# Latent attention in a two-block fp32 network: the k and q columns in turn, half of them inside the head loop, and the rope tables made one stage earlier

## The chip, the cores and the metric

One core of one Trainium2 chip. The metric is the device time of one execution, in microseconds (us), median of the runs shown. TensorE (PE) runs matmuls and transposes; VectorE (DVE), ScalarE (ACT) and GpSimd (POOL) do the rest of the arithmetic; SyncE (SP) issues the loads of weights.

## The reference

Two transformer-like blocks on 512 tokens of width 1024, all in fp32. The first is retention with a pooling mixer and a convolutional FFN. The second has two layers: an S5 state space mixer with a SwiGLU FFN (here "the second FFN", stage f2), then latent attention with another SwiGLU FFN (stage f3). The change is in the attention and in f2. What the attention computes:

```python
def mla_shared_kv(h, w_kv_a, kv_a_norm, w_kv_b, k_nope_norm, k_rope_norm, cos, sin):
    ckv = h @ w_kv_a                                        # 512 x (256 + 32)
    c_kv = rms_norm(ckv[..., :KV_LORA_RANK], kv_a_norm)
    k_rope = apply_rope(rms_norm(ckv[..., KV_LORA_RANK:], k_rope_norm), cos, sin)
    kv = (c_kv @ w_kv_b).reshape(bsz, seq, N_HEADS, QK_NOPE_DIM + V_DIM)    # 16 heads, 64 + 64
    k_nope = rms_norm(kv[..., :QK_NOPE_DIM], k_nope_norm)
    v = kv[..., QK_NOPE_DIM:]
...
def mla_queries(h, w_q_a, q_a_norm, w_q_b, q_nope_norm, q_rope_norm, cos, sin):
    c_q = rms_norm(h @ w_q_a, q_a_norm)                     # 512 x 384
    q = (c_q @ w_q_b).reshape(bsz, seq, N_HEADS, QK_DIM)    # 16 heads, 64 + 32
    q_nope = rms_norm(q[..., :QK_NOPE_DIM], q_nope_norm)
    q_rope = apply_rope(rms_norm(q[..., QK_NOPE_DIM:], q_rope_norm), ...)
...
# causal softmax attention per head, then x = x + o @ w_o, then the SwiGLU FFN
```

The angles of the rope tables depend on the input positions, so cos and sin are made on the chip.

## The kernel before

**Split products.** Every fp32 product is made of three matmuls: each operand is split into a high part, rounded to the fp32r format, and the low rest; PE adds high x high, high x low and low x high. Weights come in chunks of up to 1024 columns per partition: SP loads a chunk into one of six slots of `w_raw` (L891 to L895), ScalarE rounds it into `w_hi` (L936, and L931 scales it by a norm's gain for kv_a and q_a), GpSimd makes `w_lo` (L865). ScalarE has no list of its own for the chunks: `ahead(count)` (L921) makes them up to four past the chunk that the next result to be read belongs to, so a chunk waits when ScalarE waits for something else. SP waits for the slot's last user, six chunks back. GpSimd takes chunks in order and has one other job in this stage, the rotation of q of groups 0 and 2 (`rope_queries`, L853), put behind a given chunk (L868).

**Order.** Each engine has its own program in order. PE's order rules: every product or transpose opens the next of eight PSUM banks in turn (`open_bank`, L311) and waits until the one that had it eight openings before was released. The engines wait for each other by semaphores alone.

**The stage around the change.** After f2 the rows are normalised and transposed (stage "mla", L1208 and L1832). Then, in PE's order (L719 to L785):

- kv_a (288 columns, four token blocks one after the other, `rows_by_tile`, four chunks of two row blocks) and q_a (384 columns, four chunks, `rows_product`). VectorE first makes the angles of the rope tables (L1833 to L1840, helpers to L1463) and ScalarE their Sin (L1210 to L1212). VectorE then copies each result into SBUF (L1842, L1851), ScalarE takes Square, sum and Sqrt of the copy (L1213 to L1228), VectorE scales it (L1845 to L1857).
- The latents are transposed (`turn_rows`, L724 and L727), multiplied by a gain, split into `a_hi` and `a_lo` (L1229, L1230; L1858, L1859). VectorE makes `q_trig` (L1861) and the shared rope part of k (L1869 to L1879).
- kv_b: four column groups of 512, one for four heads each; then q_b: four groups of 384 (L729 to L735). A group is 24 or 36 matmuls in four banks. For each group and token block (i = 0 to 31), ScalarE writes Square into one of two buffers `sq` and copies k or q out (L1258, L1260); VectorE sums the squares and, for kv, copies v (L1916 to L1923). When a group's sums are there, ScalarE takes the Sqrt (`row_deviations`, L1232) and VectorE normalises the group (`normalised(n)`, L1881); for q it waits for GpSimd's rotation or does the rotation itself (groups 1 and 3, L833). Both are called a few steps into the next group.
- The head loop (L774 to L785). Heads 0 and 1 are transposed (`head_turn`, which waits for `qk_rows`, the count of normalised groups), head 0 gets its scores. Then for each head h and token block t PE does the scores of head h + 1 and the transposes of the probabilities of head h; then `head_turn(h + 2)` and `head_out(h)`. That opens eleven banks a head. VectorE masks and takes the maximum (L1935), copies three of four transposed blocks (L1950), the k of head h + 2 (L1928), and divides the output (L1958); ScalarE takes Exp (L1274), copies the fourth block (L1290) and the q of head h + 2 (L1269).
- The output `o_n` is transposed and multiplied by `w_o`.

In f2, the gate and value columns of step f are two products of 24 matmuls; VectorE multiplies them in `swiglu` (L1816), ScalarE takes Silu (L1029).

## Time and profile before

| | us |
|---|---|
| median of 3 runs (1954.29 to 1962.46) | 1956.29 |
| the profiled execution | 1960.23 |
| its span, first to last instruction | 1958.4 |
| PE busy | 1821.8 (93%) |
| DVE busy | 814.4 (42%) |
| ACT busy | 651.4 (33%) |
| POOL busy | 679.7 (35%) |

The mean granted clock of TensorE is 0.96 of full speed. The profile names engines by the short names in brackets above; PEld is PE's weight load. A row of a timeline has the start, the duration, the engine, the line, the operation with output <- input and shape, how many were merged (x4), and in brackets the idle time of that engine before it with what ended it. A matmul's duration includes its way through the array; the next one starts before it is over, so the distance between two starts is what it costs. Row durations of DVE, ACT and POOL overlap by some 0.1 us as well.

### The profile page before, as it was taken

To read this page: it belongs to the slowest core of one execution; us is meant where nothing else is said; L and a number is where in the kernel's file an instruction comes from. 1 tells how busy PE (TensorE), PEld (TensorE's weight loads), DVE (VectorE), ACT (ScalarE), POOL (GpSimd) and SP (SyncE) were. 2 spreads that over 40 slices of the span, in tenths; PEclk is the share of its full clock that TensorE was granted. 3 is DMA by queue.
4 is the path that set the end of the run, shared out by engine and by line. 5 is a ranking of instruction groups with operands and counts; after the bars stand their busy time and mean duration, and the time that the engine had idled before them with its cause. 6 is when DMAs were issued, how large, how long until landed. Compare 5 with 4: busy or idle time off the path is not lost.

```text
span 1958.4 us, 22658 instructions
## 1 busy us (share of the span) xinstructions
PE 1821.8 (93%) x9038; PEld 1522.5 (78%) x9038; DVE 814.4 (42%) x1445; ACT 651.4 (33%) x1102; POOL 679.7 (35%) x300
## 2 busy tenths in 40 slices
PE   6789999999999589999999999998879999999999
PEld 5677787788787468878988888877858898888887
DVE  1587579769755524522311110125676331111111
ACT  1223135335253232232422222236555343223121
POOL 1432234434343330024344344423510134534442
PEclk8899999999999788999999999998989999999999
DMA  9221234454545344622333323212300133333322
GB/s 214 60 76 55 86 90 152 125 164 134 166 121 167 115 151 153 238 89 86 98 97 97 97 86 108 92 57 80 93 1 1 44 87 97 96 97 92 102 91 81
DMA packets 234215, 202.71 MB, mean 104 GB/s; under 512 B 38912, under 2 KB 194688, under 8 KB 232064
## 3 DMA queue, kind: packets, MB, share of 16 engines
q1 hardware_dynamic: 198272, 170.29, 28.5%
q10 hardware_dynamic: 35840, 30.98, 5.2%
q8 instruction: 73, 1.20, 0.3%
q14 instruction: 30, 0.25, 0.0%
HBM read 175.55 MB, written 25.69 MB: 103 GB/s over the span
## 4 chain that ended last, share of the span: by engine, by line
PE 75%; DVE 14%; DMA 3%; ACT 3%; ACTq 2%; issue 2%; POOL 1%; SPq 1%; DVEq 0%; POOLq 0%
PE ps L347 11%; PE ps L349 11%; PE ps L348 11%; PE ps L371 9%; PE ps L373 9%; PE ps L372 9%; DMA rec<-s_records 2%; PE ps L750 2%; PE ps L769 2%; PE ps L402 1%; PE ps L404 1%; PE ps L403 1%; PE ps L666 1%; DVE x_rows L1437 1%; PE ps L760 1%
## 5 line engine op out<-in xcount | busy, mean ns | idle before, releaser
L865 POOL TENSOR_TENSOR w_lo<-w_raw,w_hi 128x1024 fp32r<-128x1024 f32 (+4 forms) x284 | 668.7, 2365 | 1238.6 <-ACT w_hi L936 1238.3
L347 PE MATMUL ps<-a_hi,w_hi 128*128 128x512 f32 (+1 forms) x1184 | 443.7, 375 | 10.5 <-DVE q_t L1585 6.1
L348 PE MATMUL ps<-a_lo,w_hi 128*128 128x512 f32 (+1 forms) x1184 | 441.8, 373 | 0.0
L349 PE MATMUL ps<-a_hi,w_lo 128*128 128x512 f32 (+1 forms) x1184 | 441.7, 373 | 0.0
L936 ACT ACTIVATE w_hi<-w_raw 128x1024 fp32r<-128x1024 f32 (+4 forms) x284 | 283.8, 1016 | 320.2 <-DMA w_raw<-in_ffn_w_gate_up_dram 72.8
L347 PEld LDWEIGHTS ps<-a_hi,w_hi 128*128 128x128 f32 x1184 | 224.0, 189 | 51.8 <-issue 6.8
L349 PEld LDWEIGHTS ps<-a_hi,w_lo 128*128 128x128 f32 x1184 | 223.9, 189 | 39.0
L348 PEld LDWEIGHTS ps<-a_lo,w_hi 128*128 128x128 f32 x1184 | 223.9, 189 | 38.7
L371 PE MATMUL ps<-w_hi,a_hi 128*128 128x512 f32 (+1 forms) x432 | 172.1, 398 | 39.3 <-POOL w_lo L865 18.8
L1821 DVE TENSOR_TENSOR ev<-ps,xh 128x512 f32<-128x512 f32 x44 | 30.4, 692 | 417.4 <-PE ps L349 407.4
L371 PE MATMUL ps<-w_hi,h_hi 128*128 128x512 f32 x476 | 190.4, 400 | 9.0 <-DVE x_rows L1410 4.9
L373 PE MATMUL ps<-w_hi,h_lo 128*128 128x512 f32 x476 | 189.2, 397 | 0.0
L372 PE MATMUL ps<-w_lo,h_hi 128*128 128x512 f32 x476 | 189.2, 397 | 0.0
L372 PE MATMUL ps<-w_lo,a_hi 128*128 128x512 f32 (+1 forms) x432 | 170.4, 394 | 0.0
L373 PE MATMUL ps<-w_hi,a_lo 128*128 128x512 f32 (+1 forms) x432 | 170.2, 394 | 0.0
L1410 DVE TENSOR_TENSOR x_rows<-ps,x_rows 128x512 f32<-128x512 f32 x72 | 49.2, 691 | 233.4 <-PE ps L373 193.3
L371 PEld LDWEIGHTS ps<-w_hi,a_hi 128*128 128x128 f32 x432 | 86.0, 199 | 56.2 <-issue 24.7
L371 PEld LDWEIGHTS ps<-w_hi,h_hi 128*128 128x128 f32 x476 | 90.1, 189 | 33.0 <-issue 8.1
L952 ACT ACTIVATE h_hi<-ev 128x512 fp32r<-128x512 f32 x66 | 41.5, 629 | 209.7 <-DVE ev L1821 195.5
L373 PEld LDWEIGHTS ps<-w_hi,h_lo 128*128 128x128 f32 x476 | 90.1, 189 | 21.8
L372 PEld LDWEIGHTS ps<-w_lo,h_hi 128*128 128x128 f32 x476 | 90.2, 190 | 21.3
L373 PEld LDWEIGHTS ps<-w_hi,a_lo 128*128 128x128 f32 x432 | 85.4, 198 | 15.1
(334 smaller groups left out, 2241.9 us busy)
## 6 DMA issues: line engine op xcount, KB each, us to landing
w_raw<-in_ffn_w_gate_up_dram SPq DMA_DIRECT2D x88, 512.0 KB, 3.8
rec<-s_records ACTq DMA_DIRECT2D x16, 1440.0 KB, 6.3
w_raw<-in_w_up_dram SPq DMA_DIRECT2D x44, 512.0 KB, 4.0
w_raw<-in_ffn_w_down_dram SPq DMA_DIRECT2D x40, 512.0 KB, 3.6
s_records<-stage SPq DMA_DIRECT2D x16, 928.0 KB, 6.2
w_raw<-in_w_in_dram SPq DMA_DIRECT2D x20, 512.0 KB, 4.1
w_raw<-in_w_down_dram SPq DMA_DIRECT2D x20, 512.0 KB, 4.2
w_raw<-in_ssm_w_glu_dram SPq DMA_DIRECT2D x16, 512.0 KB, 3.6
```

Source lines behind the costliest of these rows:

```text
L347: pe.matmul(bank, wh, xh_, start=first, stop=False)
L348: pe.matmul(bank, wh, xl_, start=False, stop=False)
L349: return pe.matmul(bank, wl, xh_, start=False, stop=last)
L371: pe.matmul(o, ah[:, k + kk, s], wh[:, kk, :], start=(n == 0 and kk == 0), stop=False)
L372: pe.matmul(o, ah[:, k + kk, s], wl[:, kk, :], start=False, stop=False)
L373: m = pe.matmul(o, al[:, k + kk, s], wh[:, kk, :], start=False, stop=end)
L750: m = pe.matmul(b[:, 0:(t + 1) * P], qk_t[:, h % 2, 0, t * P:t * P + P], qk_t[:, h % 2, 1, 0:(t + 1) * P], start=True, stop=True)
L769: m = pe.matmul(b[:, t * VD:t * VD + VD], p_t[:, o:o + P], v_n[:, j, h, :], start=(j == 0), stop=(j == t))
L865: pool.tensor_tensor(w_lo[:, n % RING, 0:w], w_raw[:, n % RING, 0:w], w_hi[:, n % RING, 0:w].bitcast(F), ALU.subtract).then_inc(lo_made, 1)
L936: act.activation(w_hi[:, n % RING, 0:w], w_raw[:, n % RING, 0:w], ACT.Copy).then_inc(hi_made, 1)
L952: act.activation(hi, view(ev[:, i % 2, :]), ACT.Copy).then_inc(hi_ready, 1)
L1410: ins = v.tensor_tensor(o, b, o, ALU.add)
```

## The change

- kv_a is taken in chunks of three row blocks. Its and q_a's results are read from PSUM by ScalarE and VectorE, without the copies in between.
- The angles are made by VectorE in f2 before step 4, Sin by ScalarE before step 6, and `q_trig` by VectorE before step 10. The shared rope part of k is made after the sums of kv_b's group 0.
- kv_b and q_b are taken in turn, group by group; groups 0 and 1 before the heads. Groups 2 and 3 are cut into 16 pieces of one token block (`column_piece`), in the order kv 2, q 2, kv 3, q 3; two of them in each of heads 0 to 7, the first after the second score block, the second before `head_out`. A head with pieces opens thirteen banks. ScalarE's evictions and VectorE's sums follow suit; the Sqrt of a late group comes in heads 2, 4, 6 and 8 ahead of the first piece's eviction, its normalisation at the end of the same head.
- `head_turn(h)` waits for the two normalised groups of its own four heads and those before.
- GpSimd rotates q of group 0 behind the third chunk after q_b 0, and q of group 2 behind the next one.
- The latents lie in blocks 0 to 4 of `a_hi` and 3 to 7 of `a_lo`, and `o_n` is laid out by pairs of heads over the other blocks.

```diff
+EARLY = 2
+PIECES = 2
...
-            rows_by_tile(("kv_a",), mla_w_kv_a_2, a_hi, a_lo, KT, 0, KVR + ROPE, 2, gain=0, wait_t=mla[1],
+            rows_by_tile(("kv_a",), mla_w_kv_a_2, a_hi, a_lo, KT, 0, KVR + ROPE, 3, gain=0, wait_t=mla[1],
...
+            for c in range(EARLY):
+                columns(0, c)
+                columns(1, c)
...
+            def column_piece(i):
+                n, t = divmod(i, TT)
+                if n >= 2 * HC:
+                    return
+                c, q = divmod(n, 2)
+                nk, cn, at_k = (QR // P, HN * QK, 2) if q else (KVR // P, HALF, 0)
+                w = mla_w_q_b_2[0] if q else mla_w_kv_b_2
+                b = open_bank(((("kv_b", "q_b")[q]), c, t))
+                if t == 0:
+                    piece_parts[:] = [take_chunk(rows_of(w, k, min(2, nk - k), c * cn, cn), min(2, nk - k), cn)
+                                      for k in range(0, nk, 2)]
...
             def head_turn(h):
-                pe.wait_ge(qk_rows, HC + h // HN + 1)
+                pe.wait_ge(qk_rows, 2 * (h // HN + 1))
...
                     head_probs(h, t)
+                    if t == 1:
+                        column_piece(2 * EARLY * TT + PIECES * h)
                 if h + 2 < NH:
                     head_turn(h + 2)
+                column_piece(2 * EARLY * TT + PIECES * h + 1)
                 head_out(h)
...
-                    if n == chunks_at[("q_b", c, 0)] + 2:
+                    if n == chunks_at[("q_b", c, 0)] + (3 if c < EARLY else 1):
                         rope_queries(c)
...
+                        if (stage, f) == ("f2", 6):
+                            rope_trig()
...
+            for i in range(2 * EARLY * TT):
+                evict_piece(i)
+                if i % TT == 1 and i > TT:
+                    row_deviations(i // TT - 1)
...
                     if h + 1 < NH:
                         exponentials(h + 1, t)
+                n, t = divmod(2 * EARLY * TT + PIECES * h, TT)
+                if t == 0 and 2 * EARLY < n <= 2 * HC:
+                    row_deviations(n - 1)
+                evict_piece(2 * EARLY * TT + PIECES * h)
                 if h:
                     act.wait_ge(*closed(("o", h - 1)))
                 b = full(act, ("pt", h, TT - 1))
                 release(("pt", h, TT - 1), act.activation(p_t[:, tri(TT - 1)], b, ACT.Copy))
                 if h + 2 < NH:
                     q_turned(h + 2)
+                evict_piece(2 * EARLY * TT + PIECES * h + 1)
...
+                        if (stage, f) == ("f2", 4):
+                            rope_angles()
+                        if (stage, f) == ("f2", 10):
+                            rope_factors()
...
             for t in range(TT):
-                w = release(("q_a", t), v.tensor_copy(cq[:, t, :], full(v, ("q_a", t))[:, 0:QR]))
-                v.wait_ge(*w)
-                v.memset(st[:, 190:191], 0.0).then_inc(lat_in, 1)
-            for t in range(TT):
-                v.wait_ge(lat_dev, TT + t + 1)
+                b = full(v, ("q_a", t))
+                v.wait_ge(lat_dev, 2 * TT + t + 1)
                 step(v.reciprocal(st[:, 48 + t:49 + t], st[:, 40 + t:41 + t]))
-                v.tensor_scalar(cq[:, t, :], cq[:, t, :], st[:, 48 + t:49 + t], None, ALU.mult).then_inc(cq_ready, 1)
+                release(("q_a", t), v.tensor_scalar(cq[:, t, :], b[:, 0:QR], st[:, 48 + t:49 + t], None, ALU.mult))
...
+            for i in range(2 * EARLY * TT):
+                piece_sums(i)
+                if i % TT == 2 and i > TT:
+                    normalised(i // TT - 1)
+                if i == TT - 1:
+                    k_rope()
...
-            normalised(2 * HC - 1)
+            normalised(2 * EARLY - 1)
...
+                piece_sums(2 * EARLY * TT + PIECES * h)
                 if h + 2 < NH:
                     k_turned(h + 2)
...
                 v.wait_ge(*w)
+                piece_sums(2 * EARLY * TT + PIECES * h + 1)
+                n, t = divmod(2 * EARLY * TT + PIECES * h, TT)
+                if t == 0 and 2 * EARLY < n <= 2 * HC:
+                    normalised(n - 1)
```

## Rows read from the trace of the kernel before

**Rows 1.** Busy time in stretches: engines (instructions), then granted clock, DMA share, GB/s.

```profile
1310.53:1445.42 134.89, 104.10 (x539) 93.83 (x538) 83.80 (x209) 75.74 (x186) 54.20 (x34) 0.86 0.23 70
1445.42:1531.60 86.18, 86.18 (x619) 72.88 (x618) 57.69 (x193) 47.52 (x136) 0.00 (x0) 1.00 0.01 2
```

**Rows 2.** Timeline of DVE, second FFN: start, duration, work, [idle before <- releaser].

```profile
1022.58 0.69 DVE L1821 TENSOR_TENSOR ev<-ps,xh 128x512 f32<-128x512 f32 x1 [9.59 <-PE ps L349]
```

**Rows 3.** Timeline of PE, 1310 to 1445 us, where it had been idle.

```profile
1316.13 0.37 PE L402 MATMUL ps<-w_hi,a_hi 128*128 128x288 f32 x1 [2.78 <-ACT w_hi L936]
...
1334.16 0.66 PE L371 MATMUL ps<-w_hi,a_hi 128*128 128x384 f32 x1 [3.80 <-POOL w_lo L865]
...
1359.58 0.77 PE L371 MATMUL ps<-w_hi,a_hi 128*128 128x512 f32 x1 [3.63 <-DVE ev L1356]
...
1399.68 0.66 PE L371 MATMUL ps<-w_hi,a_hi 128*128 128x384 f32 x1 [3.20 <-POOL w_lo L865]
...
1430.10 5.03 PE L750 MATMUL ps<-qk_t 96*128 96x128 f32 x10 [13.21 <-issue]
...
1441.34 0.61 PE L742 MATMUL ps<-ident,q_n 128*96 128x128 f32 x4 [2.52 <-ACT prob L1274]
```

**Rows 4.** Busy time and granted clock (1.00 is full) right after two restarts.

```profile
1316.74:1320.01 3.27, 2.86 (x13) 2.53 (x12) 1.20 (x2) 0.30 (x1) 0.83 (x1) 0.52 0.02 5
1400.14:1405.58 5.44, 5.44 (x19) 5.44 (x19) 2.40 (x4) 0.00 (x0) 4.53 (x3) 0.50 0.04 12
```

**Rows 5.** Timelines of POOL, PE and ACT: prices of one instruction.

```profile
1314.58 1.41 POOL L865 TENSOR_TENSOR w_lo<-w_raw,w_hi 128x576 fp32r<-128x576 f32 x1 [12.16 <-ACT w_hi L936]
...
1387.13 0.33 PE L372 MATMUL ps<-w_lo,a_hi 128*128 128x384 f32 x1
1387.30 0.33 PE L373 MATMUL ps<-w_hi,a_lo 128*128 128x384 f32 x1
...
1374.49 0.38 ACT L1258 ACTIVATE xh<-ps 128x256 f32<-128x256 f32 x1 [0.29 <-PE ps L373]
1374.77 0.38 ACT L1260 ACTIVATE k_n<-ps 128x256 f32<-128x256 f32 x1
1375.85 0.38 ACT L1258 ACTIVATE xh<-ps 128x256 f32<-128x256 f32 x1 [0.70 <-PE ps L373]
...
1354.12 1.04 ACT L936 ACTIVATE w_hi<-w_raw 128x1024 fp32r<-128x1024 f32 x1
...
1392.23 1.48 POOL L837 TENSOR_TENSOR q_rot<-q_n,q_trig 128x256 f32<-128x256 f32 x1 [6.06 <-ACT q_n L1260]
```

**Rows 6.** Timeline of ACT: a table load and the Sqrt behind it.

```profile
1328.32 1.28 ACT L1219 ACT_TABLE_LOAD   x1
1329.62 0.30 ACT L1219 ACTIVATE st<-st,eps_c 128x1 f32<-128x1 f32 x1
```

**Rows 7.** Timeline of DVE: the last normalisation of a q group.

```profile
1435.86 1.23 DVE L1896 TENSOR_TENSOR q_n<-q_n,xh 128x1024 f32<-128x1024 f32 x1
1437.00 0.42 DVE L837 TENSOR_TENSOR q_rot<-q_n,q_trig 128x256 f32<-128x256 f32 x1
...
1439.75 0.69 DVE L1903 TENSOR_TENSOR q_n<-q_n,xh 128x512 f32<-128x512 f32 x1
```

**Rows 8.** Timelines of PE and ACT in a settled head.

```profile
1464.55 0.44 PE L750 MATMUL ps<-qk_t 96*128 96x128 f32 x2
...
1466.57 1.02 PE L750 MATMUL ps<-qk_t 96*128 96x512 f32 x2
...
1468.74 2.34 PE L769 MATMUL ps<-v_n,p_t 128*128 128x64 f32 x20
1470.92 0.44 PE L750 MATMUL ps<-qk_t 96*128 96x128 f32 x2
...
1468.42 0.69 ACT L1274 ACTIVATE prob<-ps,st 128x512 f32<-128x512 f32 x1 [0.65 <-DVE st L1935]
...
1469.10 0.59 ACT L1290 ACTIVATE p_t<-ps 128x512 f32<-128x512 f32 x1
```

More of the change, by code:

```diff
@@ L193, in program @@
         rot = scratch("rot", [P, 2, NH, ROPE // 2], F, 81)
-        o_n = nc.alloc_sbuf_tensor_at("o_n", [P, TT, NH * VD], F, offset=base + 32 * KB)
+        o_n = nc.alloc_sbuf_tensor_at("o_n", [P, NH // 2, TT, 2 * VD], F, offset=base + 26 * KB)
+        c_hi, c_lo = a_hi[:, 0:5, :], a_lo[:, 3:8, :]
         qk_t = scratch("qk_t", [QK, 2, 2, SEQ], F, 64)
@@ L725, in _ @@
                       ready=lambda t: pe.wait_ge(ckv_ready, t + 1), through_ev=True)
-            kv_split = n_split[0] - TT
+            cq_split = n_split[0]
             turn_rows("cq_t", lambda t, k: cq[:, t, k * P:k * P + P], QR // P,
-                      ready=lambda t: pe.wait_ge(cq_ready, t + 1), through_ev=True)
-            for c in range(HC):
-                rows_product(("kv_b", c), mla_w_kv_b_2, a_hi, a_lo, KVR // P, c * HALF, HALF, 2,
-                             wait_t=(lambda t, k: kv_split + t + 1) if c == 0 else None)
@@ L732, in _, with columns @@
-            pe.wait_ge(lo_ready, n_split[0])
-            for c in range(HC):
-                rows_product(("q_b", c), mla_w_q_b_2[0], a_hi[:, 2:5, :], a_lo[:, 2:5, :], QR // P,
-                             c * HN * QK, HN * QK, 2)
+                      ready=lambda t: pe.wait_ge(*freed[bank_no[("q_a", t)]]), through_ev=True)
+            def columns(q, c):
+                if q:
+                    rows_product(("q_b", c), mla_w_q_b_2[0], c_hi[:, 2:5, :], c_lo[:, 2:5, :], QR // P,
+                                 c * HN * QK, HN * QK, 2, wait_t=(lambda t, k: cq_split + t + 1) if c == 0 else None)
+                else:
+                    rows_product(("kv_b", c), mla_w_kv_b_2, c_hi, c_lo, KVR // P, c * HALF, HALF, 2,
+                                 wait_t=(lambda t, k: kv_split + t + 1) if c == 0 else None)
@@ new lines, in _ @@
+            for c in range(EARLY):
+                columns(0, c)
+                columns(1, c)
+            piece_parts = []
+            def column_piece(i):
[9 more added lines that the diff above has]
+                                      for k in range(0, nk, 2)]
+                for k, (wh, wl) in zip(range(0, nk, 2), piece_parts):
+                    kn = min(2, nk - k)
+                    for kk in range(kn):
+                        s = slice(t * P, t * P + P)
+                        end = k + kk == nk - 1
+                        ah, al = c_hi[:, at_k + k + kk, s], c_lo[:, at_k + k + kk, s]
+                        pe.matmul(b[:, 0:cn], ah, wh[:, kk, :], start=(k + kk == 0), stop=False)
+                        pe.matmul(b[:, 0:cn], ah, wl[:, kk, :], start=False, stop=False)
+                        m = pe.matmul(b[:, 0:cn], al, wh[:, kk, :], start=False, stop=end)
+                    if t == TT - 1 and not end:
+                        chunk_over(m)
+                over = close_bank(((("kv_b", "q_b")[q]), c, t), m)
+                if t == TT - 1:
+                    chunk_done.append(over)
```

136 lines of the change are left out of this document (66 added, 70 removed).

## The prediction

> **What bounds the kernel now.** I read the busy time of the engines in stretches first. Between 1310.53 us, where the transposes of the third token block for the attention part begin, and 1445.42 us, where the loop over heads has settled, PE is busy for 104.10 of 134.89 us, so 30.8 us are idle; from there to 1531.60 us it has no idle time at all, at a granted clock of 1.00 [rows 1]. Elsewhere the change touches only the second FFN, where VectorE idles 9.59 us in each column step [rows 2]. So the question is how much of the 30.8 us goes and what the settled loop gives back.
>
> The timeline of PE shows where it is idle [rows 3]: 2.78 us before the third chunk of kv_a, 3.80 before q_a, 3.63 before kv_b, 3.20 inside q_b behind GpSimd's w_lo, 13.21 before the first scores, then 2.52; the small rest is 1.7. After each of the first five PE runs at the lower of its two clock levels. 3.27 us at a granted 0.52 after the first lose 3.27 x 0.48 = 1.6 us, 5.44 us at 0.50 after the fourth lose 2.7 [rows 4]; I take 1.6 each for the second and third too, and half of the 5.03 us of ten scores after the fifth [rows 3], 2.5. Together 10.0 us. Idle and slow time come to 40.8 us: **kv_a** 3.2 + 1.6 = 4.8, **q_a** 3.8 + 1.6 = 5.4, **kv_b** 4.1 + 1.6 = 5.7, **q_b** 3.2 + 2.7 = 5.9, **start of the heads** 16.5 + 2.5 = 19.0. PE's work itself is the same in both kernels: the same products and transposes, in another order. So the sum is 40.8 less what idle and slow time remain.
>
> **The change part by part.**
> *kv_a in chunks of three.* ScalarE makes two chunks before the norm of this stage, now six of eight row blocks. PE lasts 2.4 us on them (18 matmuls of 288 columns, estimated at 0.13 us from the 0.17 of 384 [rows 5]). The last chunk is made where the third was: its w_lo ends with the row at 1314.58 and its 1.41 us [rows 5], at 1316.0. PE waits 2.1 us instead of 3.2, under the 2.52 us that cost no clock [rows 3]. Remains 2.1.
>
> *Rope tables into the second FFN, kv_a and q_a read from PSUM.* In the old place VectorE made the angles before it copied kv_a, and ScalarE waited behind it with the weight chunks of q_a queued: that is the 3.80 us. Now the q_a chunks are split while kv_a runs, and nothing remains. In the FFN, some 3 us of small VectorE work fall into the 9.59 us [rows 2]; on ScalarE two table loads of 1.28 us [rows 6] and two Sin; PE is five banks and four weight chunks ahead there, so I cost it at nothing. Without that cover it would be 3 to 6 us. SP and GpSimd are moved past nothing here.
>
> *The latents.* The copies of q_a out of PSUM go, but Square, Sqrt, scaling, gain and split still follow q_a's last matmul in series, and kv_b's four banks need four gain steps. The wait shrinks by 0.4 us. Remains 3.7 + 1.6 = 5.3.
>
> *k and q of a group in turn.* The 3.20 us were GpSimd's rotation queued ahead of the weight split for q_b. It now comes after the split of the second group's last chunk and starts when q_b of group 0 is evicted; PE has 11.6 us of kv_b and q_b of group 1 to run by then (24 matmuls of 1.36/6 = 0.227, 36 of 0.173 [rows 5]). Remains nothing. The rotation itself takes 5.6 us, six steps of which the first is the row at 1392.23 [rows 5].
>
> *Start of the heads.* PE does groups 0 and 1 in 2 x (5.4 + 6.2) = 23.2 us, 25.2 with the slow start. Counting VectorE from kv_b's start: latents split 5.1; sums and v of kv_b to 7.9; the shared rope key (3.3) when the last tile is in, to 12.1; q_b 0 and the first normalisation to 17.1; kv_b 1, then q of group 0, which waits for GpSimd until 20.9, to 23; q_b 1, k of group 1 and two k_turned to 29.4. PE is ready for scores at 27.0: wait 1.7. Then q of group 1 is normalised on VectorE: 1.2 + 6 x 0.44 + 0.7 and reciprocals = 5.0 us [rows 7], with masks of head 1 behind it. With the extra piece in the bank order, the last transpose of head 0 needs a bank that head 1's first exp frees: PE waits 2.7 us at 34.7, and before the output of head 0 another 1.9 for head 1's last exp, the split of a weight chunk (1.04 us [rows 5]) and the piece's eviction. Remains 6.3 instead of 19.0.
>
> *Pieces in heads 0 to 7.* PE has 16 pieces more there (1.36 us for kv, 36/4 x 0.173 = 1.55 for q), moved, not added. A settled head takes 6.37 us of PE, and its tightest chain is scores from 1466.57, mask, exp at 1468.42, copy of p_t 1469.10 to about 1469.6, against the last part of the output at 1469.8 [rows 8]: 0.3 us to spare. A piece adds 1.4 us of cover, but the output's bank is the one of the head's first piece, so it waits for that eviction: exp, Square, Copy (0.28 us apart [rows 5]), on kv also VectorE's sum and copy. That is 2.7 us after the last scores against 2.67 of PE work: no wait in a plain head. In heads 2, 4, 6 and 8 ScalarE first takes the Sqrt of the row sums. That needs another table. The load takes 1.28 us and Sqrt follows 0.02 us later [rows 6]; with the Sqrt itself 1.6 us for k, 1.95 for q. It stands before the eviction, and in heads 2, 4 and 6 a weight split of 0.95 (1.04 less the overlap with its neighbour), or 0.75 for a smaller chunk, stands there too. Waits: head 2 1.9, head 4 (kv, through VectorE) 2.9, head 6 2.0, head 8 1.7. VectorE's normalisations add after head 4 (2.1 us) 1.2, and after head 8 (5.0, with its own rotation [rows 7], no piece to cover) 4.0. Sum **13.7**. The load back to the Exp table falls beside the output product and I cost it at nothing; uncovered it would be 1.3 in each of four heads. Three waits of 2.7 and more may cost clock, as 2.78 did [rows 3, 4]: some 1.0 each, **3.0**. This case's trace never shows Sqrt between Exps, nor eviction between heads. Bounds: all of it hidden, 0, as the settled loop's idle time is [rows 1]; double the waits, 33.4. I take 16.7, as it is counted from rows near by.
>
> A page of the Trainium skill speaks against the change: ScalarE: Activation LUTs, section What ACT_TABLE_LOAD costs, has a drain of about 1.38 us beside each load, 2.66 us for a switch. By that the four switches in the heads would cost 5.5 us more, and the time would be 1951.4. The 0.02 us from load to Sqrt [rows 6] speak for the load alone.
>
> *The o_n layout and the use of other blocks of a_hi and a_lo* change addresses only; same sizes, same counts: nothing. SP's queue has the chunks of kv_b and q_b in another order and one chunk fewer; each is asked for six chunks ahead.
>
> **Sum.** Remaining: 2.1 + 0 + 5.3 + 0 + 6.3 + 16.7 = 30.4; gain 40.8 - 30.4 = 10.4 us. The profiled execution took 1960.23 us, 1.8 more than its span and 3.9 above the median of 1956.29. It would take 1949.8; against the median, 1945.9.
>
> **The rivals.**
> A, *the heads hide it all*: PE has 2.9 us more per head and the other engines run ahead. For: no idle time from 1445.42 to 1531.60 [rows 1]; against: 0.3 us to spare [rows 8]. Gain 27.1, time 1929.2. Chance 0.22.
> B, *given back*: waits in the heads twice as long (ordinary heads wait 0.5 to 1 us for the bank too, the load back to Exp isn't hidden). 1945.9 + 16.7 = 1962.6. Chance 0.15.
> C, *slower*: the output of each of the eight piece heads waits for the whole serial chain of mask, exp, eviction, sum and copy, 3.3 us, plus a weight split of 1, with nothing beside it. 8 x 4.3 = 34.4, less the 8.0 that I count in heads 2, 4, 5 and 6: 1945.9 + 26.4 = 1972.3. It decides from 3.5 us a head on: 8 x 3.5 - 8.0 = 20.0, which is what lies between the forecast and 0.5% above the median, 1966.1. For: the tight chain; against: evictions are pipelined 0.28 us apart [rows 5]. Chance 0.06.
> D, *a table switch costs more than its load*: if ScalarE stood idle around a switch once more for as long as the load takes, 1.28 us [rows 6], that would come four times on the chain of the heads, 5.1 us, 1951.0. For: the row is a switch after a Square, not after an Exp; against: it shows a gap of 0.02. Chance 0.04. The page on the activation tables, named above, makes that wait 1.38.
> That the change doesn't do what it says is excluded by its loops: all eight pieces of each late group are issued in heads 0 to 7.
>
> **How the numbers follow.** The forecast has 0.53, between 1938 and 1956 by its unknown terms. To leave out no more than 2 in 10, the range goes to A below, a little past its middle, and to half of B above: 1928 to 1961. A change under 0.5% (9.8 us) can't be told from none here; the bound is 1946.5, and the forecast lies on it. Faster: 0.22 of A and 0.31 of the forecast, 0.53. Same: 0.22 of the forecast, B and D, 0.41. Slower: 0.06.
>
> **What would show it.** PE idle before q_a and inside q_b gone, at most 2.2 us in kv_a, some 3.6 still before kv_b; the wait before the first scores 1 to 3 us instead of 13.21; heads 1, 3 and 7 about 9.2 us apart without idle time; table loads in heads 2, 4, 6 and 8, with PE idle 1.7 to 3 us before the output product; a wait of some 3 us in head 9. No new wait in the second FFN. The forecast is wrong if the settled heads with pieces show idle time everywhere, or the Sqrt heads none.

## The result, and the profile after

The kernel with the change takes **1967.37 us** (median of 13 runs, 1962.25 to 1974.71), the kernel before 1956.29 (13 runs, 1950.51 to 1962.46): a ratio of 1.0059 with a 95% interval of 1.0043 to 1.0075. It is slower by about 11 us. I had forecast 1945.9 and a range of 1928 to 1961.

The profiled execution took 1962.25 us. The page of the kernel after, its span, busy times and two of the lines in 40 slices:

```profile
span 1960.4 us, 22648 instructions
...
PE 1825.8 (93%) x9038; PEld 1522.4 (78%) x9038; DVE 809.0 (41%) x1433; ACT 657.6 (34%) x1107; POOL 676.9 (35%) x299
...
PE   6789989999998599999999999999888999999999
...
PEclk8899999999999788999999999999889999999999
```

The page says little: 93% busy, as before, and three slices at 8 where the heads are. And the whole time is a poor measure here, because the part of the program ahead of the attention varies by itself: kv_a's first matmul starts at 1311.52 us in the profile of before, at 1303.42 in that of after, and between 1300.34 and 1311.27 in the profiles of the experiments, of which only one touches that part (rope tables back). So I measure **the stage**: from kv_a's first matmul to the first matmul of w_o. Busy time in that stretch, before and then after with its parts (columns as in [rows 1]):

```profile
1311.52:1542.87 231.35, 199.04 (x1229) 175.04 (x1229) 146.17 (x414) 128.59 (x334) 54.20 (x34) 0.92 0.14 43
```

```profile
1303.42:1544.83 241.41, 210.33 (x1229) 181.31 (x1229) 136.54 (x383) 132.91 (x335) 49.51 (x33) 0.91 0.13 40
1303.42:1376.74 73.32, 62.20 (x357) 58.31 (x357) 42.49 (x96) 45.19 (x116) 30.70 (x20) 0.95 0.28 78
1376.74:1393.88 17.14, 15.13 (x67) 11.00 (x67) 11.56 (x34) 8.42 (x24) 0.00 (x0) 0.80 0.00 1
1393.88:1451.93 58.05, 47.40 (x246) 39.92 (x246) 23.61 (x74) 26.17 (x65) 11.77 (x10) 0.82 0.09 28
1451.93:1508.00 56.07, 50.28 (x297) 41.17 (x298) 36.60 (x111) 33.62 (x79) 7.04 (x3) 0.91 0.09 29
1508.00:1544.83 36.83, 35.31 (x269) 30.91 (x267) 22.29 (x70) 19.51 (x52) 0.00 (x0) 1.00 0.04 15
```

The same 1229 matmul rows, 241.41 us against 231.35: the stage is 10.1 us longer, which is the result. Idle time fell a little (32.3 to 31.1 us), but the matmuls themselves take 11.3 us more, at a granted clock of 0.82 and 0.91 in the two stretches that hold turns 1 to 9 of the head loop. Before, the heads ran at 1.00.

The timeline of PE where it had been idle, kernel after: first the part ahead of the heads, then the heads.

```profile
1308.03 0.37 PE L403 MATMUL ps<-w_hi,a_hi 128*128 128x288 f32 x1 [1.99 <-POOL w_lo L905]
...
1321.94 0.41 PE L372 MATMUL ps<-w_hi,a_hi 128*128 128x384 f32 x1 [0.95 <-DVE ckv L1917]
...
1371.31 0.64 PE L779 MATMUL ps<-ident,q_n 128*96 128x128 f32 x4 [0.78 <-DVE q_n L1963]
1376.74 4.93 PE L787 MATMUL ps<-qk_t 96*128 96x128 f32 x10 [3.48 <-ACT qk_t L1317]
1387.88 0.63 PE L797 MATMUL ps<-ident,prob 128*128 128x128 f32 x4 [1.19 <-ACT prob L1322]
1391.60 2.44 PE L806 MATMUL ps<-v_n,p_t 128*128 128x64 f32 x20 [0.81 <-DVE v_n L1984]
...
1414.32 4.47 PE L806 MATMUL ps<-v_n,p_t 128*128 128x64 f32 x20 [1.88 <-ACT q_n L1304]
...
1436.46 0.77 PE L765 MATMUL ps<-w_hi,a_hi 128*128 128x512 f32 x1 [5.83 <-POOL w_lo L905]
...
1448.04 4.11 PE L806 MATMUL ps<-v_n,p_t 128*128 128x64 f32 x20 [2.92 <-DVE v_n L1984]
...
1472.73 2.44 PE L806 MATMUL ps<-v_n,p_t 128*128 128x64 f32 x20 [2.10 <-ACT q_n L1304]
...
1492.02 1.18 PE L806 MATMUL ps<-v_n,p_t 128*128 128x64 f32 x8 [1.83 <-ACT p_t L1342]
```

Beside these stand the wait before kv_b (3.78 us) and three under 0.9 in head 9. Of the waits of [rows 3], the 3.80 before q_a shrank to 0.95, the 3.20 inside q_b is gone, the 13.21 before the first scores is 3.48. In heads 2, 4, 6 and 8 PE waits 1.88, 2.92, 2.10 and 1.83 us before the output product, where I had counted 1.9, 2.9, 2.0 and 1.7. And there is one that I had not: **5.83 us in head 4, behind GpSimd's w_lo**. The timeline of POOL just before it:

```profile
1429.24 0.73 POOL L877 TENSOR_TENSOR q_rot<-q_n,q_trig 128x256 f32<-128x256 f32 x1 [55.36 <-ACT q_n L1304]
...
1433.29 0.73 POOL L882 TENSOR_TENSOR q_n<-q_n,q_rot 128x256 f32<-128x256 f32 x1
1433.97 5.08 POOL L905 TENSOR_TENSOR w_lo<-w_raw,w_hi 128x1024 fp32r<-128x1024 f32 x3
```

GpSimd stood idle for 55.36 us, rotated q of group 2 once ScalarE had evicted its last piece, and only then split the weights of kv_b group 3, for which PE was waiting. `rope_queries(2)` stands behind chunk `chunks_at[("q_b", 2, 0)] + 1`, and that is the last chunk of q_b 2 itself, ahead of kv_b 3's. PE couldn't go on to the scores of head 5, so VectorE and ScalarE waited too (the row at 1441.33 below, 9.04 us). The timeline of ScalarE, around the Sqrt of head 2 and behind that stall:

```profile
1411.17 1.28 ACT L1282 ACT_TABLE_LOAD   x1
1412.47 0.31 ACT L1282 ACTIVATE xh<-xh,eps_c 128x16 f32<-128x16 f32 x1
1412.68 0.83 ACT L976 ACTIVATE w_hi<-w_raw 128x768 fp32r<-128x768 f32 x1
1413.41 0.47 ACT L1302 ACTIVATE xh<-ps 128x384 f32<-128x384 f32 x1
1413.78 0.48 ACT L1304 ACTIVATE q_n<-ps 128x384 f32<-128x384 f32 x1
...
1419.40 1.28 ACT L1322 ACT_TABLE_LOAD   x1 [3.33 <-PE ps L787]
...
1441.33 0.58 ACT L1322 ACTIVATE prob<-ps,st 128x384 f32<-128x384 f32 x1 [9.04 <-DVE st L2002]
```

The order is the one that I had written down: load, Sqrt, weight split, Square, Copy, which frees the bank. The gap from load to Sqrt is 0.02 us again, and the load back to the Exp table falls beside the first scores, before the mask that the Exp needs.

### The profile page after: what moved, and what is told of

It is laid out like the page before. It is cut to its first block, busy times and chain, and to the rows that moved or that the text cites. A ratio compares the mean times of both kernels' runs of the same rounds, so it can differ in the third digit from the quotient of the medians.

```text
span 1960.4 us, 22648 instructions
## 1 busy us (share of the span) xinstructions
PE 1825.8 (93%) x9038; PEld 1522.4 (78%) x9038; DVE 809.0 (41%) x1433; ACT 657.6 (34%) x1107; POOL 676.9 (35%) x299
## 4 chain that ended last, share of the span: by engine, by line
PE 76%; DVE 12%; ACT 4%; DMA 3%; issue 2%; ACTq 2%; POOL 1%; SPq 1%; DVEq 0%; POOLq 0%
PE ps L348 12%; PE ps L349 12%; PE ps L350 12%; PE ps L372 8%; PE ps L373 8%; PE ps L374 8%; DMA rec<-s_records 2%; PE ps L806 2%; PE ps L787 2%; PE ps L403 1%; PE ps L405 1%; PE ps L404 1%; PE ps L667 1%; DVE x_rows L1490 1%; ACT w_hi L976 1%
## 5 line engine op out<-in xcount | busy, mean ns | idle before, releaser
L348 PE MATMUL ps<-a_hi,w_hi 128*128 128x512 f32 (+1 forms) x1184 | 443.9, 375 | 10.9 <-DVE q_t L1638 6.6
L372 PE MATMUL ps<-w_hi,a_hi 128*128 128x512 f32 (+1 forms) x392 | 155.0, 395 | 34.3 <-DVE a_lo L1399 12.9
L373 PE MATMUL ps<-w_lo,a_hi 128*128 128x512 f32 (+1 forms) x392 | 154.1, 393 | 0.0
L374 PE MATMUL ps<-w_hi,a_lo 128*128 128x512 f32 (+1 forms) x392 | 153.8, 392 | 0.0
L372 PEld LDWEIGHTS ps<-w_hi,a_hi 128*128 128x128 f32 x392 | 76.4, 195 | 50.3 <-issue 18.9
L374 PEld LDWEIGHTS ps<-w_hi,a_lo 128*128 128x128 f32 x392 | 76.4, 195 | 14.2
```

What stands on the lines that cost most here:

```text
L348: pe.matmul(bank, wh, xh_, start=first, stop=False)
L372: pe.matmul(o, ah[:, k + kk, s], wh[:, kk, :], start=(n == 0 and kk == 0), stop=False)
L373: pe.matmul(o, ah[:, k + kk, s], wl[:, kk, :], start=False, stop=False)
L374: m = pe.matmul(o, al[:, k + kk, s], wh[:, kk, :], start=False, stop=end)
```

## The experiments

Each median is of 6 or 12 runs (13 for the first two rows), in three groups with the kernel before beside them (medians of before 1955.57, 1956.42 and 1956.18 us); the ratio is to that of the group. "Stage" is the stretch defined above, "front" the part of it up to the first scores, and "turns" the part from the start of turn 1 of the head loop to w_o; a turn of the loop is called a head. The front shifts by 1.5 us from one profile to the next with nothing changed in it (q_a starts 17.0 or 18.5 us after kv_a; the early ones are marked *). What shifts is the clock: behind the first wait in kv_a, 1.99 us in both, PE ran at a granted 0.82 in the kernel after and at 1.00 in the next run:

```profile
1303.42:1312.80 9.38, 7.39 (x43) 7.19 (x43) 2.21 (x4) 5.75 (x11) 3.24 (x2) 0.82 0.31 87
1300.34:1308.22 7.88, 5.89 (x44) 5.68 (x44) 2.21 (x4) 5.76 (x11) 3.25 (x2) 1.00 0.33 103
```

The turns are free of this shift but not of others like it, as head 1 shows below, so a difference of one profile is good to 2 or 3 us at best. The stage is that of one profiled execution each: the median is the firmer number, and the difference of two medians can be 7 us away from that of the stages.

| kernel | median us | ratio (95% interval) | front | turns | stage | clock in stage |
|---|---|---|---|---|---|---|
| before | 1956.29 |  | 118.58 | 97.45 | 231.35 | 0.92 |
| after | 1967.37 | 1.0059 [1.0043, 1.0075] | 73.32 | 150.95 | 241.41 | 0.91 |
| rotation behind kv 3 | 1957.06 | 1.0012 [0.9994, 1.0031] | 71.80 * | 140.92 | 229.95 | 0.93 |
| Sqrt last | 1947.55 | 0.9965 [0.9947, 0.9983] | 73.31 | 137.06 | 227.50 | 0.93 |
| no table load in heads | 1944.90 | 0.9942 [0.9923, 0.9961] | 73.30 | 133.62 | 224.17 | 0.95 |
| all groups early | 1938.86 | 0.9904 [0.9881, 0.9927] | 101.95 | 99.03 | 217.11 | 0.94 |
| three groups early | 1947.03 | 0.9951 [0.9933, 0.9969] | 87.00 * | 121.39 | 223.06 | 0.93 |
| rope tables back | 1948.62 | 0.9958 [0.9941, 0.9975] | 109.55 | 97.43 | 222.91 | 0.95 |
| kv then q | 1946.43 | 0.9948 [0.9927, 0.9968] | 105.55 | 100.51 | 222.26 | 0.93 |
| late normalisation | 1937.79 | 0.9903 [0.9879, 0.9926] | 100.12 | 103.68 | 212.83 | 0.97 |
| pieces mended | 1947.20 | 0.9950 [0.9929, 0.9970] | 73.32 | 132.13 | 220.17 | 0.95 |
| late, and all rotations on GpSimd | 1932.55 | 0.9876 [0.9849, 0.9903] | 95.19 * | 102.01 | 206.23 | 0.99 |

**Rotation behind kv 3.** The changed kernel, with GpSimd's rotation of group 2 one chunk later:

```diff
-                    if n == chunks_at[("q_b", c, 0)] + (3 if c < EARLY else 1):
+                    if n == chunks_at[("q_b", c, 0)] + (3 if c < EARLY else 2):
```

> Edit: GpSimd rotates q of group 2 behind the weight split of kv_b's group 3 instead of ahead of it; nothing else. Measure: the time, and the stage from the first matmul of kv_a to the first of w_o, which took 231.4 us before and 241.4 with the change. Theory Q (queue order): in head 4 PE waited 5.83 us for that split behind the rotation, then ran at the low clock, and head 4 took 22.5 us against 9.1 of work; with the order mended that wait goes, head 4 takes 12 to 15 us, the stage 231 to 234, the time 1956 to 1960, ratio to before 1.000 to 1.002. Theory T (table loads and evictions bound the heads, the rotation's wait only came first): another wait takes its place in head 4, the stage stays over 238 and the time over 1963.

The stage fell from 241.41 to 229.95 us (231 to 234 expected). The 5.83 us wait is gone; heads 1 to 5, which took 11.1 13.6 10.8 **22.5** 11.2, became 9.4 12.4 12.1 **14.1** 11.2. Head 4 loses 8.4 us: the wait and 2.6 us of slow clock. The turns lose 10.0 (150.95 to 140.92), but the other 1.6 lies in heads 1 to 3, and heads 1 and 2 the edit doesn't reach. Head 1, the same instructions without a wait, in the kernel after and in this run:

```profile
1393.88:1404.93 11.05, 11.03 (x60) 8.87 (x60) 5.62 (x18) 4.62 (x14) 0.00 (x0) 0.85 0.11 25
1389.37:1398.81 9.44, 9.43 (x61) 7.61 (x60) 5.54 (x18) 4.62 (x14) 0.00 (x0) 1.00 0.10 27
```

The medians agree with the larger figure, 1967.37 to 1957.06 us. So a position in a queue that is wrong by one chunk is what makes the change a loss; with it mended the change is worth nothing either way, within the interval.

**Sqrt last.** On top of that, the Sqrt of a late group goes behind both evictions of its head, so that it stands ahead of nothing that PE waits for; the normalisation follows one head later.

```diff
-                n, t = divmod(2 * EARLY * TT + PIECES * h, TT)
-                if t == 0 and 2 * EARLY < n <= 2 * HC:
-                    row_deviations(n - 1)
...
                 evict_piece(2 * EARLY * TT + PIECES * h + 1)
+                n, t = divmod(2 * EARLY * TT + PIECES * h, TT)
+                if t == 0 and 2 * EARLY < n <= 2 * HC:
+                    row_deviations(n - 1)
```

> Edit: as e1, and in heads 2, 4, 6, 8 ScalarE takes the Sqrt of the row sums after both evictions and the copies of the head, VectorE normalises the group one head later. The same instructions, the two table loads included, but not ahead of the eviction that frees the output's bank. Theory T1 (the load costs by its place on the chain): the waits of 1.9, 2.9, 2.1 and 1.8 us before the output products go, and the slow clock behind the first two; 6 to 14 us less than e1, stage 219 to 227, ratio 0.994 to 0.997. Theory T2 (ScalarE is simply too full in these heads, wherever the loads stand): they come back as a wait for the first Exp of the next head, and the gain over e1 is under 3 us.

The median is 9.5 us lower and its ratio 0.9965, as theory T1 has it; the turns of the profile are only 3.9 us shorter and the stage 2.4. The split by heads explains the difference. Heads 2 to 8 take 10.5 us less and now run at full clock; heads 9 to 11 take 6.6 more (30.6 against 24.0), where a wait of 3.23 us in head 10 stands behind the last normalisation, which comes one head later and holds VectorE ahead of the masks. Heads 2 to 8 with the rotation behind kv 3, then in this run, then in the next one without table loads:

```profile
1398.81:1478.98 80.17, 71.12 (x420) 61.22 (x419) 42.20 (x132) 48.70 (x113) 14.77 (x12) 0.91 0.11 37
1404.31:1473.98 69.67, 64.61 (x420) 54.78 (x420) 42.82 (x133) 46.51 (x111) 15.60 (x12) 1.00 0.13 43
1401.03:1470.44 69.41, 64.41 (x421) 54.77 (x420) 42.30 (x133) 39.28 (x106) 14.79 (x12) 1.00 0.13 43
```

The waits before the output product fell, from 1.89 to 0.25 us in head 2, from 2.92 to 1.71 in head 4, from 2.08 to 1.29 in head 6 and from 1.83 to 0.81 in head 8. ScalarE at the end of head 2:

```profile
1413.85 1.28 ACT L1282 ACT_TABLE_LOAD   x1
1415.14 0.31 ACT L1282 ACTIVATE xh<-xh,eps_c 128x16 f32<-128x16 f32 x1
1415.47 1.28 ACT L1322 ACT_TABLE_LOAD   x1
1416.77 0.37 ACT L1322 ACTIVATE prob<-ps,st 128x128 f32<-128x128 f32 x1
```

Both loads now stand in front of the next head's Exp, which follows without idle time on ScalarE. PE waits for nothing in head 3 all the same (9.5 us), so theory T2 is not borne out.

**No table load in the heads.** Rotation behind kv 3, and Identity in place of Sqrt for the late groups, so the kernel leaves out the root in the norms of heads 8 to 15.

```diff
+                fn = ACT.Sqrt if n < 2 * EARLY else ACT.Identity
```

> Edit: as e1, but the Sqrt of the late groups (heads 2, 4, 6, 8) is left out: Identity with the same scale and bias in its place, which needs no table load, so the row norms of heads 8 to 15 are not the reference's. The waits fall to the Sqrt's own 0.3 us. Theory T: at least as fast as e2 if place is all; if e3 is faster than e2 by over 3 us, the loads cost something wherever they stand; if e3 gains under 3 us on e1, the loads never mattered and the low clock has another cause. I expect e3 6 to 15 us under e1, within 3 us of e2.

The turns take 7.3 us less than with the rotation mended (133.62 against 140.92), 1.8 for each of four switches. That is a net: heads 2 to 8 take 10.8 us less, and heads 9 to 11 give 3.5 back, in and behind a wait of 3.61 us in head 9, where VectorE normalises q of the last group ahead of the masks. In heads 2 to 8 leaving the loads out gives no more than moving them (69.41 against 69.67 us). So what costs there is their place ahead of the eviction, not the loads by themselves; by the medians the two kernels are 2.7 us apart, within the 3 that I expected. With the switches gone about half of what the pieces cost in the stage (next run) is still there.

**All groups early.** The changed kernel with `EARLY = 4`: no pieces, everything else of the change stays.

```diff
-EARLY = 2
+EARLY = 4
```

> Edit: the change with all four groups before the heads (EARLY = 4), so no pieces and no Sqrt in the head loop; k and q in turn, rope tables in the second FFN and PSUM reads stay. This is the front part of the change alone. My sum gave the front 2.7 + 5.4 + 0.4 + 5.9 us and a shorter start of the heads. Theory F (the front part gains, the pieces lose it): the stage takes 211 to 222 us and the ratio is 0.990 to 0.995. Theory G (the front saves nothing, since VectorE is behind and takes it back at the start of the heads): stage 228 or more, ratio over 0.998, with a wait of over 10 us before the first scores.

The stage is 217.11 us, 14.2 less than before, and the time 1938.86, 17 us less. This separates the change into a front that wins 14.2 us and pieces that cost 12.8 us (229.95 - 217.11) even with the queue mended, 14.3 with the shift of the front taken out, and 18.2 by the medians (1957.06 and 1938.86). Head 1 takes 8.0 us and all later ones 6.4.

**Three groups early.** `EARLY = 3`, pieces in heads 0 to 3 alone, Sqrt in heads 2 and 4.

> Three of the four column groups ahead of the heads, only the fourth as pieces, in heads 0 to 3; the rotation of group 2 then also stands behind the next group's weight splits. From the first kv_a matmul to the first one of w_o the kernel with two early groups and the order mended needs 229.95 us, the one with all four early 217.11. Theory (each piece and each Sqrt among Exps has its price): about half of the 12.8 us between them, 222 to 225 us, and 1945 to 1948 us in all; no head longer than 12.5 us behind head 1. Rival 1 (the price lies in the start, where the other engines lag and pieces come on top): 226 or more, 1949 or more. Rival 2 (what costs is that many heads in a row stay irregular and PE's clock low): under 220, under 1943.

The stage is 223.06 us (224.6 without the shift of the front), the time 1947.03: half the pieces cost half, 7.5 of 14.3 us, or 8.2 of 18.2 by the medians. The price goes with the number of pieces and switches, as the first theory says; its "no head longer than 12.5" failed, head 2 takes 13.9, after a wait of 2.09 us at a low clock.

**Rope tables back.** All groups early, with `rope_angles`, `rope_trig` and `rope_factors` called where the kernel before does that work.

```diff
-                        if (stage, f) == ("f2", 4):
-                            rope_angles()
-                        if (stage, f) == ("f2", 10):
-                            rope_factors()
...
             rms_and_split("mla", 2 * TT, to_a, add_last("f2"))
+            rope_angles()
```

> All four groups early, and the rope tables put back to where the kernel before has them: VectorE makes the angles ahead of its kv_a work, ScalarE its two Sin behind the split of the third stage, the factors behind the split of the latents. Theory (my step: the wait before q_a, 3.80 us and its low clock 1.6, comes from these tables): the wait before q_a goes from 0.97 back to about 4 us, the stretch from kv_a to w_o from 217.1 to 221 to 223 us, in all 1942.5 to 1945. Rival (it came from the copies of kv_a out of PSUM and the changed chunks, not from the tables): under 219 us, within 1.5 us of 1938.9.

The stage grows by 5.8 us, and PE's wait before q_a from 0.97 to 6.84:

```profile
1326.25 0.66 PE L372 MATMUL ps<-w_hi,a_hi 128*128 128x384 f32 x1 [6.84 <-DVE ckv L1913]
```

I had the term at 5.4 (3.8 and 1.6 of clock). The near agreement with 5.8 is in part luck. Up to kv_b's first matmul this run is 7.8 us later, 5.9 by the wait and 1.9 by the clock behind it; 2.0 in sum come back further on, by the clock: behind a wait of 2.43 us before a kv_b group it stays at 1.00, where all groups early had 0.76 behind 2.44, and head 1 runs at full clock, where it had 0.80. The median is 9.8 us above that of all groups early, 1948.62 against the 1942.5 to 1945 expected. Why the wait is longer than the 3.80 of [rows 3] I didn't test; the row names VectorE's scaling of kv_a, which now reads PSUM and frees the bank.

**kv then q.** All groups early, all of kv_b ahead of all of q_b.

```diff
-            for c in range(EARLY):
-                columns(0, c)
-                columns(1, c)
+            for q in range(2):
+                for c in range(EARLY):
+                    columns(q, c)
```

> All four groups early, but all four of kv_b first and then all four of q_b, as in the kernel before; GpSimd's rotation stays behind the weight splits of the next q group. This takes back the order alone. Theory (the order of k and q in turn gives VectorE and GpSimd time for q while PE runs kv_b): VectorE waits for the rotations with no kv_b between, and scores start 3 to 8 us later than the 101.95 us after kv_a's first matmul, the stretch to w_o is 220 to 226 us, in all 1942 to 1948. Rival 1 (the order does nothing; what the kernel before lost was GpSimd's queue and the latents): scores at 100 to 103, 215 to 219 us, 1937 to 1941. Rival 2 (the order is the whole gain): scores at 112 or later, 227 or more, 1949 or more.

The stage is 5.2 us longer, the median 7.6. The two waits before kv_b groups (1.75 and 2.44) vanish, but the one before the scores is 13.46, as large as in [rows 3]:

```profile
1412.80 1.62 PE L787 MATMUL ps<-qk_t 96*128 96x128 f32 x4 [13.46 <-issue]
```

```profile
1395.63 0.97 DVE L877 TENSOR_TENSOR q_rot<-q_n,q_trig 128x256 f32<-128x256 f32 x1
...
1401.01 2.71 DVE L1963 TENSOR_TENSOR q_n<-q_n,xh 128x512 f32<-128x512 f32 x1
...
1411.96 1.40 DVE L1995 TENSOR_SCALAR qk_t<-ps,gcol 96x512 f32<-96x512 f32 x2
```

VectorE has the sums and normalisations of three q groups in a row and is 12 us behind PE when it comes to the k of head 0. With the order alone taken back, the 13.21 us return: it is k and q in turn that makes that wait small, for 4.2 us of waits further ahead.

**Late normalisation.** All groups early; the last three of the eight normalisations go behind the outputs of heads 1, 3 and 5, and GpSimd rotates group 3 too.

```diff
-                if i % TT == 2 and i > TT:
+                if i % TT == 2 and TT < i < 6 * TT:
                     normalised(i // TT - 1)
...
-                n, t = divmod(2 * EARLY * TT + PIECES * h, TT)
-                if t == 0 and 2 * EARLY < n <= 2 * HC:
-                    normalised(n - 1)
+                if h in (1, 3, 5):
+                    normalised(5 + h // 2)
```

> All four groups early; the normalisation of the last three of the eight row sets (q of group 2, k and q of group 3) is taken out of the start and put behind the outputs of heads 1, 3 and 5 on VectorE, and GpSimd rotates group 3 too. Theory (VectorE is what PE waits for from kv_b to the first scores: 1.75, 2.44 and 3.38 us): scores start 5 to 8 us earlier than 101.95, three heads get some 1 to 2 us longer, and the stretch to w_o is 210 to 214 us, 1932 to 1936 us in all. Rival (the masks of the heads behind a normalisation come late and PE waits as long there as before, at a low clock): 216 to 220 us, 1938 to 1942.

The stage is 212.83 us, 4.3 less. The median, 1937.79, lies between the two forecasts and only 1.1 below that of all groups early, so it doesn't confirm the gain. The scores start only 1.8 us earlier, not 5 to 8: the waits of 1.73 and 2.45 us before kv_b groups are still there, since they come from earlier normalisations. The gain is the first head, 16.1 to 9.0 us, where q of the last group had stood ahead of the masks of head 1. Heads 2, 3, 4 and 6 get 0.9 to 1.9 longer.

**Pieces mended.** Sqrt last, and q of group 1 normalised behind the output of head 0, with all four rotations on GpSimd.

```diff
-                for c in range(0, HC, 2):
-                    if n == chunks_at[("q_b", c, 0)] + (3 if c < EARLY else 2):
+                for c in range(HC):
+                    if n == chunks_at[("q_b", c, 0)] + (3, 3, 2, 1)[c]:
...
-            normalised(2 * EARLY - 1)
...
+                if h == 0:
+                    normalised(2 * EARLY - 1)
```

> Pieces of groups 2 and 3 in heads 0 to 7 as in the changed kernel, with three things mended: the rotation of group 2 behind the next group's weight split, Sqrt behind both evictions (that much is the run with Sqrt last, 227.50 us from kv_a to w_o, first head 17.1 us), and now q of group 1 normalised behind the output of head 0 instead of ahead of it, with all rotations on GpSimd. Theory (the 17.1 us of the first head, against 9.3 of PE work in it, come from VectorE's normalisation of q of group 1 ahead of the masks of head 1): first head 9.5 to 12 us, two or three later ones a little longer, 219 to 223 us, 1940 to 1944 us in all; still above the 217.11 of all groups early. Rival 1 (the first head waits for ScalarE's exps, pieces and weight splits, whatever VectorE does): first head 15 us or more, 226 or more. Rival 2 (with the stalls gone the pieces hide the waits that all groups early has, and win): under 217.

The stage is 220.17 us, as expected, but the first head takes 14.7 (17.1 before the edit), near the first rival's 15. It is not that rival's wait: PE is busy for 14.70 of the 14.72 us, at a granted clock of 0.78. The time, 1947.20, is above the expected 1940 to 1944 and equal to the 1947.55 of Sqrt last, so the medians don't confirm the gain of the stage. The best form of the pieces that I tried stays behind all groups early, by 3 us of the stage and 8 of the medians; against the next run, which has the same mends and no pieces, it is 14 and 15.

**Late, and all rotations on GpSimd.** Late normalisation, and GpSimd also rotates group 1.

```diff
-                for c in (0, 2, 3):
+                for c in range(HC):
...
-                    if c == 1:
-                        go(rope_chunk(v, c, q_rot[:, 1, :, :, :, :], step))
-                    else:
-                        v.wait_ge(q_roped, (1, 0, 2, 3)[c])
+                    v.wait_ge(q_roped, c + 1)
```

> All four groups early with the late normalisation (212.83 us from kv_a to w_o, scores at 100.12), and GpSimd rotates group 1 as well, which VectorE did itself. Theory (VectorE is what PE waits for between kv_b and the scores: 1.73, 2.45 and 1.62 us): the 2.45 us before the last kv_b group shrinks to under 1, 210 to 212 us, 1935 to 1938 in all. Rival (GpSimd's rotation slows VectorE beside it and holds up the weight splits, so that the wait only changes its releaser): 212.5 to 216.

The 2.45 us wait is down to 0.55, the scores start 4.9 us earlier (1.5 of that is the shift of the front), one more head is at 6.4. Better than expected, and **the fastest kernel of the study: 1932.55 us, 0.9876 of the kernel before**, with PE at a granted clock of 0.99 in the whole stage:

```profile
1308.89:1515.12 206.23, 190.11 (x1229) 167.36 (x1229) 133.76 (x371) 122.64 (x327) 61.24 (x45) 0.99 0.15 46
```

## Why the prediction was wrong

I had the stage 10.4 us shorter; it is 10.1 longer, 20.5 us between. The runs and the trace split that:

| where | predicted | measured | miss |
|---|---|---|---|
| front, to the first scores | 69.5 | 73.32 | 3.9 |
| first head | 17.0 | 17.14 | 0.1 |
| heads after it, beyond the moved products: GpSimd's queue, in head 4 | 0 | 8.4 | 8.4 |
| the same: all else | 16.7 | 24.7 | 8.0 |

(Front: 118.58 less 23.2 for the groups moved and less the 25.9 gained by my terms up to there. First head: 15.3 before, less its 5.8 idle and slow, plus the 4.6 of waits that I counted and 2.9 for two pieces at the mean price of both sorts. Heads after it: the turns took 97.45 before; 14 pieces take 20.4 more; after has 150.95 and so 33.1 extra; head 4 gives back 8.4 with the queue mended, and the turns in all 10.0, to 140.92, so 23.1 extra there.)

**The step that failed: "Remains nothing" for GpSimd's rotation.** I checked that the rotation of group 0 now stands behind the second group's weights and let that stand for both. For group 2 the code says `+ 1` where group 0 has `+ 3`. I described that position and didn't cost it. One question would have found it: for a step that is moved, what is behind it on its queue, and who waits for that? Behind it were kv_b 3's weights, due in the same head. The price could be had: 5.6 us for the six rotation steps, as I counted them for group 0, and a w_lo of 1.41 or more [rows 5] behind the eviction, 7 to 8 us less the little that PE has left to do. The wait was 5.83 us, and head 4 took 8.4 more with it than without.

**The clock in the heads was mis-sized.** My waits were right one by one: 8.73 us measured in heads 2, 4, 6 and 8 against 8.5. For the clock behind them I had 3.0 us in all. By the stretches above the heads lose 58.05 x 0.18 + 56.07 x 0.09 = 15.5 us to it, and in the run with the queue mended the 23.1 are some 10.7 of idle time, 10.9 of slow clock and 1.5 that the pieces themselves take beyond my price (head 1 of that run, at full clock and without a wait, has 9.44 - 6.37 = 3.07 us for two kv pieces, where I had 2.7). I took 2.52 us as harmless from [rows 3]; here two waits of 1.88 and 2.92 us were each followed by an output product at half clock. In sum idle time in the heads cost about twice its length. With the Sqrt moved behind the evictions the clock came back too: heads 2 to 8 ran at 1.00 with 5 us of waits left in them.

**The front** missed 3.9: 1.8 more before the first scores, 0.95 before q_a where I had nothing, 0.78 before the transposes, and 1.5 of slow clock behind the wait in kv_a, for which I had none. These come to 5.0; smaller errors the other way make up the difference. One row that lies on that path is VectorE's scaling of the rotated q, which takes four times as long as in [rows 7] when it starts beside GpSimd's weight split (below).

**What was right.** The tables: 5.4 predicted, 5.8 measured by putting them back. The agreement is in part luck, as said there. The FFN takes them without a wait: from 900 to 1100 us PE is busy for 199.27 us in both kernels, while VectorE has 5.9 us more to do, where I had 3. The waits in kv_a (1.99 against 2.1) and before kv_b (3.78 against 3.7) stand.

**What was right by luck.** The first head, 17.14 against 17.0: PE waits for 2.0 us in it and not for 4.6, and the rest is a granted clock of 0.80, for which I had nothing. The waits after heads 4 and 8 were too high, 5.2 against 1.9.

**The rivals.** A (all hidden) is excluded: every Sqrt head waits. B's number for the heads, 33.4, is what the heads lost, 33.1, but not by its mechanism: no ordinary head waits, and the load back to Exp is hidden; it is one queue and the clock. C, the slower one, is as near in time (1972.3 against B's 1962.6), and its mechanism didn't happen: head 7 with its two pieces takes 9.5 us, no more than its products, and heads 1, 3 and 5 show no wait before their output product. A slower result had its place in the code, and I looked for it in the serial chain only. D: no second idle time around a load, 0.02 us in every one. The Trainium skill, ScalarE: Activation LUTs, section What ACT_TABLE_LOAD costs, has about 1.38 us of drain with each; these rows don't show it. Where ScalarE has work on both sides of a load, the gap is 0.02 us before it and 0.02 or less behind it, also between the Sqrt and the load back (rows of Sqrt last). The run without loads gives 1.8 us for a switch, but that is the net named above and no price of the load.

**The better plan for the change.** Its front is worth 14.2 us of the stage: 5.8 by the tables, 5.2 by the order of k and q. The other 3.2 (chunks of three, no copies, the queue of GpSimd) are a remainder that I didn't test; by the medians, 9.8 and 7.6 of some 17, nothing is left for it. Moving products into the heads costs 12.8 to 14.3 by the stage and 18 by the medians, and a good part of it, 7.1 by the stage and 6.0 by the medians, without any table switch: the heads as they were left PE no idle time [rows 1], so work put there adds its own time, and each wait that it brings comes on top. What the pieces were to hide, VectorE's lag at the start, is cheaper to remove by delaying VectorE's normalisations, which need no PE.

## What to carry to other kernels

When work is spread into a loop, list for every engine the queue position of each thing that moves with it, for each group and not just for the first: a helper's side job one slot too early stalls the product behind it for the whole chain. Put work into a loop only where its bound engine idles; one that is busy without a gap gains nothing and pays for each new wait, here about twice, as the clock was low behind several of them. And before moving the bound engine's work, try moving the work of the engine that it waits for.

## What the runs showed of the hardware

**Short waits and TensorE's clock.** Granted clock of five stretches of the kernel after: the output products of heads 2 and 3 (0.51 behind a wait of 1.88 us, then 1.00), the piece behind the 5.83 us, and the output products of heads 4 (2.92 us before it) and 6 (2.10 before it):

```profile
1414.32:1418.60 4.28, 4.28 (x21) 4.28 (x21) 1.07 (x3) 1.75 (x4) 0.00 (x0) 0.51 0.00 0
1427.74:1429.41 1.67, 1.67 (x17) 1.67 (x17) 0.25 (x2) 1.34 (x4) 0.17 (x1) 1.00 0.67 153
1436.46:1440.43 3.97, 3.97 (x9) 2.68 (x9) 0.00 (x0) 0.00 (x0) 2.59 (x2) 0.50 0.02 4
1448.04:1451.93 3.89, 3.89 (x20) 3.89 (x21) 0.68 (x2) 1.03 (x3) 1.32 (x1) 0.56 0.00 0
1472.73:1475.17 2.44, 2.44 (x21) 2.44 (x22) 1.07 (x3) 1.75 (x4) 1.61 (x1) 1.00 0.00 0
```

0.51 is the lower of the two levels (1.2 GHz), 1.00 the upper (2.4 GHz). The same product behind nearly the same wait, 1.88 and 2.10 us, ran once at either. Stronger still are the pairs of the section on the experiments: kv_a behind the same wait of 1.98 to 2.00 us ran at 0.82 in eight of the eleven profiles from the kernel after on, and at 1.00 in three; and head 1 had 0.85 and 1.00 with no wait in it. So the length of the wait alone doesn't decide, and a wait of this size has to be priced at both ends, its length and about twice that. I made no run that isolates what decides.

**VectorE beside GpSimd.** The scaling of the rotated q, with 512 columns from two inputs in SBUF, takes 0.69 us alone and 2.87 when it starts beside GpSimd's weight split. Kernel after, VectorE and then GpSimd:

```profile
1368.38 2.87 DVE L1963 TENSOR_TENSOR q_n<-q_n,xh 128x512 f32<-128x512 f32 x1 [0.63 <-POOL q_n L882]
...
1386.29 0.69 DVE L1963 TENSOR_TENSOR q_n<-q_n,xh 128x512 f32<-128x512 f32 x1
```

```profile
1368.31 5.57 POOL L905 TENSOR_TENSOR w_lo<-w_raw,w_hi 128x1024 fp32r<-128x1024 f32 x3
```

The sums of 256 columns, with one input, are not touched: 0.41 us beside the same weight split, 0.42 elsewhere. The Trainium skill, GPSIMD Engine Reference, section Specifications, says that GpSimd shares its SBUF interfaces with VectorE and that VectorE instructions with two SBUF inputs contend; the rows agree. They don't show a fixed factor of four, though: the first of the three splits merged in that row ends at 1370.70, and the scaling ends 0.55 us later, as it does in all groups early (split to 1373.80, scaling to 1374.35) and in kv then q (1403.17 and 1403.72). So the price here was what was left of one split, 2.2 to 2.4 us, and most of the 2.87 us looks like a wait for it; no run tests that by itself.
